# Eleven parts of a Strassen MLP take the plain eight products

## The chip, the cores and the metric

The kernel runs on one core of a Trainium2 chip. The metric is the device time of one execution in microseconds (us), lower is better. Three runs of the kernel before took 2641.0 to 2647.37 us, median 2646.51.

The core's engines each work through their own instructions in order and meet through semaphores: TensorE (PE) multiplies matrices, VectorE (DVE), ScalarE (ACT) and GpSimd (POOL) work on rows, SyncE (SP) and ACT issue DMAs.

## The reference

One layer of a decoder on 2048 prompt tokens and 64 sample tokens, width 1024: attention, then a two-layer MLP, both between norms. The part that matters here:

```python
def ffn_sublayer(x, g_pre, w_up_l, w_down_l, g_post):
    h = rmsnorm(x, g_pre)
    a = jax.nn.relu(jnp.einsum('btd,df->btf', h, w_up_l))
    return x + rmsnorm(jnp.einsum('btf,fd->btd', a * a, w_down_l), g_post)
```

`w_up` is 1024 x 4096, `w_down` 4096 x 1024. The layer's attention output `mix` goes through `w_out`, a norm, and the residual (`x1 = x + rmsnorm(mix @ w_out)`) before it.

## The kernel before, in words

Precision: every factor is split into a rounded part and its rest, `hi` and `lo`, and each product is three matmuls, hi·hi, hi·lo and lo·hi. ACT makes `hi` (a cast), DVE or POOL makes `lo` (a subtraction).

`out_and_mlp` runs after attention. It takes the tokens in four groups of 512 (the last with the 64 samples too), four tiles of 128. A group is 8 parts of 512 hidden columns. A part has:

- four units "up" (0 to 3), each 128 hidden columns: 24 matmuls, relu and square by ACT;
- then the down product of the part, 512 hidden columns x 1024 outputs, by Strassen's scheme: seven units "down" in the order P1, P7, P2, P6, P5, P4, P3. Each is two tiles x 2 blocks x 3 = 12 matmuls (L2171). Four of them need sums of the hidden blocks (`first_sums`, `second_sums`, `third_sum`, L2451, on DVE), all seven their own hi (`high`, L2266, ACT) and lo (`low`, L2479 on DVE, L1988 on POOL). P6, P7, P4 and P5 read sums of weights that an earlier stage stored as `wt`.

`steps()` is the order of all units. The first two up units of the next part stand behind P7 and P6 (`LEADS`). In a group's last part the transposes `h` of the next group's tiles (L2080, two halves each) stand behind the units 2 to 6 (`H_AT`); they and the up units share three PSUM banks (`UP_BANKS`), each to be emptied before it is used again.

Weights: SP loads the raw weights of one or two units at a time into three slots (`load_raw`). ACT's `split_hi` (L2203) and the `split_lo` of POOL (L1983) or DVE (L2485: P7, P6 and P3; in last parts P6) work two units ahead (`AHEAD`); the split weights have three slots (`SPLIT`), so a unit's hi waits until the unit three before it is used.

Sums: a product goes to one of five PSUM banks (`Y_BANKS`, chosen in `BANK`, the least recently used first; P2, P3 and P4 go on in the banks of P1, P5 and P7). DVE adds it to the group's sums (L2511 and L2513) and so frees the bank. P1 and P6 belong to two places: they are collected in `shared` and added at the start of the next group (`share`, L2534 and L2538).

Norms: between the units stand the steps of norm chains, at places given by tables (`POST`, `FIRST`, `ADD`, `PRE`, `SECOND` for the next group's `x1` and `h`; `END`, `SCALE`, `END_ADD`, `OUT` for the output of the group before). For a tile they are: ACT squares (L2275), DVE scales (L2562), POOL adds the residual (L1977), which ACT has loaded (L1864), and ACT stores it (L1870 or L2284). They lie in parts 0 to 2 of group 0 and parts 5 to 7 of groups 1 and 2 (next group), and in parts 0 and 1 of groups 1 to 3 (output). In even parts ACT also issues a copy of 3 MB from cache to cache output, behind up 3 (L118).

Unit names below: (g,p) is part p of group g.

## Time and profile before

| what | value |
|---|---|
| median of three runs | 2646.51 us |
| profiled execution | 2644.41 us, of it span 2642.6 us |
| mean granted clock of TensorE | 0.984 |
| TensorE busy with matmuls | 2522.6 us, 95% of the span |
| DVE, ACT, POOL busy | 1382.9, 1166.3, 1415.2 us |
| largest lines of the chain that ended last | `ml_y` L2171 13%, `ml_up` L2095 to L2097 8% each |
| load of `w_up`, 1024 KB: issue to landing | 6.2 us (median) |
| cache copies, 3060 KB | 11.9 and 13.2 us |

A matmul's record lasts longer than the time to the next one, as they are pipelined; the distance between two starts is what one costs. A line of a timeline has in brackets how long the engine was idle before it and what ended that. The clock is given as a share of full speed: 1.00 is 2.4 GHz, 0.5 is 1.2 GHz.

### The profile page before, as it was taken

What the parts mean: (1) busy time and instruction counts of PE and PEld (TensorE: products, weight loads), DVE (VectorE), ACT (ScalarE), POOL (GpSimd) and SP (SyncE); (2) the same over time, 40 slices, a digit from 0 to 9 for tenths busy, and PEclk for the clock granted to TensorE, in tenths of its full rate; (3) what the DMA queues carried; (4) which work ended last, traced back from release to release, by engine and by line L of the source; (5) the groups of instructions that cost most, each with busy time, mean ns of one, the idle gap of its engine ahead of it and who ended that gap; (6) DMA issues with size and microseconds to landing.
All of it is one profiled execution on the core that took longest, in us unless ns stands there. A gap on an engine that the chain in (4) does not pass through costs nothing.

```text
span 2642.6 us, 35400 instructions
## 1 busy us (share of the span) xinstructions
PE 2522.6 (95%) x13562; PEld 2167.4 (82%) x13562; DVE 1382.9 (52%) x2231; ACT 1166.3 (44%) x2002; POOL 1415.2 (54%) x818
## 2 busy tenths in 40 slices
PE   7999999999999999999998999998999999999995
PEld 6899999899996468778877788777778778889884
DVE  6431221265663225865566554676555476655657
ACT  4000110187775534545454444554544455444443
POOL 1216560068663566665566675666665475554555
PEclk9999999999999999999999999999999999999998
DMA  5316764299988944564556555456555263553452
GB/s 183 112 44 244 264 230 120 83 164 180 166 146 212 295 160 166 193 208 159 167 183 242 176 168 183 151 170 232 173 173 193 99 235 120 198 178 127 142 191 96
DMA packets 297903, 457.65 MB, mean 173 GB/s; under 512 B 81748, under 2 KB 202140, under 8 KB 290776
## 3 DMA queue, kind: packets, MB, share of 16 engines
q1 hardware_dynamic: 270546, 313.71, 41.3%
q10 hardware_dynamic: 14518, 89.43, 9.5%
q0 software_dynamic: 12672, 52.24, 5.9%
q8 instruction: 109, 1.79, 0.3%
q14 instruction: 58, 0.48, 0.1%
HBM read 390.50 MB, written 120.53 MB: 193 GB/s over the span
## 4 chain that ended last, share of the span: by engine, by line
PE 76%; DVE 10%; DMA 5%; POOL 3%; ACT 3%; issue 2%; SPq 0%; ACTq 0%; DVEq 0%; POOLq 0%
PE ml_y L2171 13%; PE ml_up L2095 8%; PE ml_up L2096 8%; PE ml_up L2097 8%; PE ml_y L2128 6%; PE pj_acc L518 6%; PE pj_acc L519 6%; PE pj_acc L520 6%; PE at_o L1187 5%; PE at_turn L1167 2%; POOL ml_w_lo L1983 2%; DVE ml_a_lo L2479 2%; DVE ml_a_lo_raw L2451 2%; DVE ml_w_lo L2485 2%; PE at_score L1156 2%
## 5 line engine op out<-in xcount | busy, mean ns | idle before, releaser
L1983 POOL TENSOR_TENSOR ml_w_lo<-em_raw,ml_w_hi 128x1024 fp32r<-128x1024 f32 x296 | 741.2, 2512 | 635.1 <-ACT ml_w_hi L2203 634.9
L2203 ACT CAST ml_w_hi<-em_raw 128x1024 fp32r<-128x1024 f32 x384 | 401.4, 1046 | 295.8 <-PE ml_y L2171 189.0
L2095 PE MATMUL ml_up<-ml_h_hi,ml_w_hi 128*128 128x512 f32 (+2 forms) x1280 | 457.1, 357 | 23.3 <-POOL ml_w_lo L1983 23.3
L2096 PE MATMUL ml_up<-ml_h_lo,ml_w_hi 128*128 128x512 f32 (+2 forms) x1280 | 453.5, 354 | 0.0
L2097 PE MATMUL ml_up<-ml_h_hi,ml_w_lo 128*128 128x512 f32 (+2 forms) x1280 | 452.6, 354 | 0.0
L2171 PE MATMUL ml_y<-ml_w_hi,ml_a_hi 128*128 128x512 f32 x896 | 358.2, 400 | 34.4 <-DVE em_hx L2513 13.8
L2171 PE MATMUL ml_y<-ml_w_lo,ml_a_hi 128*128 128x512 f32 x896 | 352.6, 393 | 0.0
L2171 PE MATMUL ml_y<-ml_w_hi,ml_a_lo 128*128 128x512 f32 x896 | 352.3, 393 | 0.0
L2095 PEld LDWEIGHTS ml_up<-ml_h_hi,ml_w_hi 128*128 128x128 f32 x1280 | 243.2, 190 | 66.3 <-POOL ml_w_lo L1983 35.3
L518 PE MATMUL pj_acc<-pj_h_hi,pj_w_hi 128*128 128x424 f32 (+1 forms) x800 | 290.3, 363 | 5.6 <-DVE pj_h_lo L736 5.6
L519 PE MATMUL pj_acc<-pj_h_lo,pj_w_hi 128*128 128x424 f32 (+1 forms) x800 | 283.5, 354 | 0.0
L520 PE MATMUL pj_acc<-pj_h_hi,pj_w_lo 128*128 128x424 f32 (+1 forms) x800 | 283.4, 354 | 0.0
L2485 DVE TENSOR_TENSOR ml_w_lo<-em_raw,ml_w_hi 128x1024 fp32r<-128x1024 f32 x88 | 132.1, 1501 | 264.7 <-ACT ml_w_hi L2203 264.4
L2096 PEld LDWEIGHTS ml_up<-ml_h_lo,ml_w_hi 128*128 128x128 f32 x1280 | 243.4, 190 | 30.7
L2097 PEld LDWEIGHTS ml_up<-ml_h_hi,ml_w_lo 128*128 128x128 f32 x1280 | 243.1, 190 | 31.0
L2171 PEld LDWEIGHTS ml_y<-ml_w_hi,ml_a_hi 128*128 128x128 f32 x896 | 170.1, 190 | 83.8 <-DVE em_hx L2513 15.7
L754 DVE SCALAR_TENSOR_TENSOR pj_proj<-pj_acc,pj_scale,pj_rstd_of 128x424 f32<-128x424 f32 (+1 forms) x100 | 65.0, 656 | 311.0 <-PE pj_acc L520 311.0
L2171 PEld LDWEIGHTS ml_y<-ml_w_hi,ml_a_lo 128*128 128x128 f32 x896 | 170.2, 190 | 36.2
L2171 PEld LDWEIGHTS ml_y<-ml_w_lo,ml_a_hi 128*128 128x128 f32 x896 | 170.5, 190 | 33.6
L2479 DVE TENSOR_TENSOR ml_a_lo<-ml_a_lo_raw,ml_a_hi 128x512 fp32r<-128x512 f32 x128 | 166.9, 1304 | 0.1
L2255 ACT ACTIVATE ml_a<-ml_up 128x512 f32<-128x512 f32 (+1 forms) x80 | 41.0, 513 | 279.4 <-PE ml_up L2097 269.6
L518 PEld LDWEIGHTS pj_acc<-pj_h_hi,pj_w_hi 128*128 128x128 f32 x800 | 150.9, 189 | 15.7 <-issue 8.3
(319 smaller groups left out, 4559.8 us busy)
## 6 DMA issues: line engine op xcount, KB each, us to landing
em_raw<-in_w_up SPq DMA_DIRECT2D x64, 1024.0 KB, 6.2
em_raw<-scratch_wt SPq DMA_DIRECT2D x128, 512.0 KB, 4.7
em_raw<-in_w_down SPq DMA_DIRECT2D x96, 512.0 KB, 3.7
out_o_a_k_s<-in_cache_a_k ACTq DMA_DIRECT2D x8, 3060.0 KB, 11.9
out_o_a_v_s<-in_cache_a_v ACTq DMA_DIRECT2D x8, 3060.0 KB, 13.2
em_raw<-scratch_pt SPq DMA_DIRECT2D x34, 512.0 KB, 7.3
pj_work<-in_w_down POOLq DMA_DIRECT2D x16, 1024.0 KB, 6.3
scratch_wt<-pj_work POOLq DMA_DIRECT2D x16, 1024.0 KB, 4.5
```

The costliest lines, as they stand in the source:

```text
L518: pe.matmul(acc[g][:, 0:n], w_hi[:, i % 2, k, :], h_hi[:, k, cols], start=(k == 0), stop=False)
L519: pe.matmul(acc[g][:, 0:n], w_hi[:, i % 2, k, :], h_lo[:, k, cols], start=False, stop=False)
L520: last = pe.matmul(acc[g][:, 0:n], w_lo[:, i % 2, k, :], h_hi[:, k, cols], start=False, stop=(k == DBLK - 1))
L1983: nc.gpsimd.tensor_tensor(split_of(w_lo, n), raw_of(n), f32(split_of(w_hi, n)), ALU.subtract).then_inc(w_lo_ready, 1)
L2095: pe.matmul(out, hi[:, k, :], h_hi[:, k, cols], start=(k == 0), stop=False)
L2096: pe.matmul(out, hi[:, k, :], h_lo[:, k, cols], start=False, stop=False)
L2097: last = pe.matmul(out, lo[:, k, :], h_hi[:, k, cols], start=False, stop=(k == DBLK - 1))
L2128: last = pe.matmul(out, p[:, f, t0:t0 + m], w[:, b, :], start=(f == 0 and p is act_hi and w is hi), stop=(f == DBLK - 1 and p is act_lo))
L2171: last = pe.matmul(out, p[:, SLOT[i], c:c + P], w[:, f, :], start=(i not in ONTO and f == 0 and p is a_hi and w is hi), stop=(f == DF - 1 ...
L2203: nc.scalar.copy(split_of(w_hi, n), raw_of(n)).then_inc(w_hi_ready, 1)
L2479: nc.vector.tensor_tensor(a_lo[:, slot, :], frm, f32(a_hi[:, slot, 0:2 * HT]), ALU.subtract).then_inc(a_lo_by_dve, 1)
L2485: nc.vector.tensor_tensor(split_of(w_lo, n), raw_of(n), f32(split_of(w_hi, n)), ALU.subtract).then_inc(w_lo_by_dve, 1)
```

## The change

In eleven parts the seven products are replaced by the plain eight: parts 0, 1 and 7 of group 0, and parts 0, 5, 6 and 7 of groups 1 and 2. Such a part is four units "plain" of 24 matmuls: unit i computes output half i // 2 from the hidden half i % 2, for all four tiles, with the sums over both hidden halves in the same PSUM banks. DVE adds four tiles after units 1 and 3. There are no sums of blocks, four hi and four lo of the hidden blocks (the lo all by DVE), and all `w_lo` are POOL's. Up units of the next part stand behind plain units 0 and 2. In last parts the `h` of the next group stand ahead of unit 0 and behind units 0, 1 and 2. The weights come as one load for two units. Norm steps keep their tables, and those placed at a product go to the plain unit given in `IN_PLAIN`. The additions of `shared` move from the next group's first up unit to up 2 and 3 of the first plain part behind the last Strassen part of a group: (0,7), (1,5), (2,5).

```diff
-    H_AT = (2, 3, 4, 5, 6)
...
+    PLAIN = ((0, 1, LAST), (0, LAST - 2, LAST - 1, LAST), (0, LAST - 2, LAST - 1, LAST), ())
+    PLAINS = 2 * DF
+    PLAIN_LEADS = (0, 2)
+    PLAIN_H = {0: (1,), 1: (2,), 2: (3, 4)}
+    PLAIN_SLOT = ((SLOT[P1], SLOT[P7]), (SLOT[P2], SLOT[P4]))
+    IN_PLAIN = {P1: 0, P7: 0, P2: 1, P6: 1, P5: 2, P4: 3, P3: 3}
+
+    def is_plain(g, part):
+        return part in PLAIN[g]
+
+    def last_of_seven(g):
+        return max(part for part in range(PARTS) if not is_plain(g, part))
+
+    def first_of_seven(g):
+        return min(part for part in range(PARTS) if not is_plain(g, part))
+
+    def sevens_before(step):
+        return sum(not is_plain(*divmod(at, PARTS)) for at in range(step[1] * PARTS + step[2]))
+
+    def plains_before(step):
+        return step[1] * PARTS + step[2] - sevens_before(step)
...
+                if is_plain(g, part):
+                    if part == LAST and g + 1 < NG:
+                        yield "h", g + 1, 0, 0
+                    for i in range(PLAINS):
+                        yield "plain", g, part, i
+                        if part < LAST and i in PLAIN_LEADS:
+                            yield "up", g, part + 1, PLAIN_LEADS.index(i)
+                        for j in PLAIN_H.get(i, ()):
+                            if part == LAST and g + 1 < NG and j < len(tiles(g + 1)):
+                                yield "h", g + 1, 0, j
+                    continue
...
+        if kind == "plain":
+            return list(range(PROMPT_TILES)) if i % DF == DF - 1 else []
...
+    def unit_at(kind, g, part, i):
+        if kind == "down" and is_plain(g, part):
+            return "plain", g, part, IN_PLAIN[i]
+        return kind, g, part, i
...
+                if kind == "plain":
+                    half = i // DF
+                    sp.dma_start(to.rearrange("p (k c) -> p k c", c=HALF),
+                                 down_v[part][:, :, half * HALF:(half + 1) * HALF]).then_inc(landed, 16)
...
+            def product_plain(n):
+                step = UNITS[n]
+                kind, g, part, i = step
+                half, f0 = divmod(i, DF)
+                wait_lo(pe, n)
+                pe.wait_ge(plain_lo, 4 * plains_before(step) + 2 * (f0 + 1))
+                hi, lo = split_of(w_hi, n), split_of(w_lo, n)
+                for j in range(PROMPT_TILES):
+                    q = sum_at(("plain", g, part, half * DF + DF - 1), j)
+                    if f0 == 0:
+                        pe.wait_ge(y_added, BEFORE[q] + 1)
+                    out, slot = y_ps[BANK[q]][:, :], PLAIN_SLOT[f0][j // PAIRS]
+                    for f in range(DF):
+                        c = f * HT + j % PAIRS * P
+                        for p, w in ((a_hi, hi), (a_hi, lo), (a_lo, hi)):
+                            last = pe.matmul(out, p[:, slot, c:c + P], w[:, f, :], start=(f0 == 0 and f == 0 and p is a_hi and w is hi),
+                                             stop=(f0 == DF - 1 and f == DF - 1 and p is a_lo))
+                    if f0 == DF - 1:
+                        last.then_inc(y_done, 1)
+                    elif j == PROMPT_TILES - 1:
+                        last.then_inc(down_used, 1)
...
-                    act.wait_ge(shared_added, PROMPT_TILES * g + j + 1)
+                    act.wait_ge(y_added, sum_at(("plain", g, LAST, PLAINS - 1), j) + 1)
...
+                        if i == DF and is_plain(g, part):
+                            act.wait_ge(y_done, FIRST_Q[step])
+                            wait_hidden(act, ("up", g, part, DF - 1))
+                            for q in range(2):
+                                high_plain(PLAIN_SLOT[0][q], a[:, q, :, :].rearrange("p f t -> p (f t)"))
...
+            def low_plain(step, his, slot, frm):
+                dve.wait_ge(plain_hi, 4 * plains_before(step) + his)
+                nc.vector.tensor_tensor(a_lo[:, slot, :], frm, f32(a_hi[:, slot, 0:2 * HT]), ALU.subtract).then_inc(plain_lo, 1)
...
+            def add_plain(step, j):
+                kind, g, part, i = step
+                q, half = sum_at(step, j), i // DF
+                dve.wait_ge(y_done, q + 1)
+                add_sum(mixed(g)[:, j, half * HALF:(half + 1) * HALF], y_ps[BANK[q]][:, :], part == 0)
...
+            def share(step):
+                kind, g, part, i = step
+                if i == DF:
+                    dve.wait_ge(y_added, FIRST_Q[step])
+                    for j in range(PAIRS):
+                        share_right(g, j)
+                else:
+                    for j in range(PAIRS):
+                        share_both(g, j)
...
-                        if g and part == 0 and i == 0:
-                            share(g - 1)
-                        if i == DF:
+                        if i == DF and is_plain(g, part):
+                            for q in range(2):
+                                low_plain(step, q + 1, PLAIN_SLOT[0][q], a[:, q, :, :].rearrange("p f t -> p (f t)"))
...
+                        if i == PF - 1 and is_plain(g, part):
+                            for q in range(2):
...
+                        if i >= DF and is_plain(g, part) and part == last_of_seven(g) + 1:
+                            share(step)
+                    elif kind == "plain":
+                        if part == last_of_seven(g) + 1 and i == DF - 1:
+                            dve.wait_ge(shared_added, PROMPT_TILES * (g + 1))
+                        for j in sums_of(step):
+                            add_plain(step, j)
```

Counters of waits that counted parts now count Strassen parts and plain parts apart.

## Rows read from the trace of the kernel before

**Rows 1.** Groups in 1040 to 2642 us: count, busy us, mean ns, idle before, releasers.

```profile
L2095 PE MATMUL ml_up<-ml_h_hi,ml_w_hi 128*128 128x512 f32 (+2 forms) x1280 | 457.1, 357 | 23.3 <-POOL ml_w_lo L1983 23.3
L2171 PE MATMUL ml_y<-ml_w_hi,ml_a_hi 128*128 128x512 f32 x896 | 358.2, 400 | 34.4 <-DVE em_hx L2513 13.8 <-DVE ml_w_lo L2485 8.7 <-DVE em_y L2513 7.6
```

**Rows 2.** Windows: stretch, span us, busy us (count) per engine, granted clock, DMA share, GB/s.

```profile
1185.02:1226.29 41.27, 41.10 (x181) 33.71 (x180) 23.52 (x26) 19.68 (x26) 22.80 (x11) 1.00 0.43 140
1042.66:1099.29 56.63, 54.06 (x229) 43.66 (x228) 34.70 (x34) 32.19 (x50) 34.44 (x14) 0.97 0.58 195
1099.29:1143.48 44.19, 41.69 (x182) 33.55 (x180) 35.16 (x34) 22.36 (x32) 30.57 (x13) 1.00 0.51 177
1350.15:1385.94 35.79, 34.11 (x165) 27.95 (x164) 25.56 (x32) 19.25 (x28) 23.42 (x11) 1.00 0.41 133
1385.94:1449.20 63.26, 55.33 (x230) 44.03 (x228) 38.66 (x39) 30.92 (x46) 38.88 (x19) 0.95 0.66 238
1666.36:1712.20 45.84, 43.33 (x182) 34.70 (x180) 34.60 (x34) 29.03 (x45) 29.88 (x12) 0.96 0.45 149
1712.20:1757.95 45.75, 43.25 (x181) 34.73 (x180) 35.02 (x34) 22.46 (x32) 30.27 (x13) 0.96 0.68 240
1757.95:1794.96 37.01, 34.41 (x166) 27.98 (x164) 26.78 (x32) 19.24 (x28) 23.41 (x11) 1.00 0.40 129
1794.96:1858.73 63.77, 55.41 (x230) 44.09 (x228) 38.66 (x39) 30.89 (x46) 38.84 (x19) 0.95 0.65 235
2085.43:2129.66 44.23, 41.71 (x181) 33.56 (x180) 35.74 (x35) 28.92 (x45) 30.07 (x12) 1.00 0.45 143
2129.66:2177.84 48.18, 43.27 (x181) 34.71 (x180) 36.87 (x36) 25.26 (x38) 33.75 (x14) 0.96 0.69 240
2177.84:2220.51 42.67, 36.81 (x173) 29.73 (x172) 32.26 (x38) 20.60 (x31) 24.35 (x11) 0.96 0.35 115
```

**Rows 3.** Timeline of TensorE: start us, us, instruction, count; clean part, then an h step.

```profile
1226.29 0.39 PE L2095 MATMUL ml_up<-ml_h_hi,ml_w_hi 128*128 128x512 f32 x1
...
1237.17 0.39 PE L2171 MATMUL ml_y<-ml_w_hi,ml_a_hi 128*128 128x512 f32 x1
...
1378.71 1.04 PE L2080 MATMUL ml_up<-all_ident,em_y 128*128 128x128 f32 x8
1379.51 0.48 PE L2171 MATMUL ml_y<-ml_w_hi,ml_a_hi 128*128 128x512 f32 x1
```

**Rows 4.** Timeline, part (0,0), DVE and TensorE: in brackets idle time before, releaser.

```profile
1078.81 3.22 DVE L2562 SCALAR_TENSOR_TENSOR em_y<-em_y,ml_rstd,ml_gain_post 128x1024 f32<-128x1024 f32 x1
...
1082.69 0.80 PE L2171 MATMUL ml_y<-ml_w_hi,ml_a_hi 128*128 128x512 f32 x1 [2.28 <-DVE em_hx L2511]
```

**Rows 5.** Timeline, part (1,0): ACT's queue, POOL, ACT, TensorE.

```profile
1410.06 0.58 ACTq L118 DMA_DIRECT2D out_o_a_k_s<-in_cache_a_k  x1
...
1413.04 0.47 ACTq L1864 DMA_DIRECT2D ml_res<-scratch_x  x1
...
1427.62 2.34 POOL L1977 TENSOR_TENSOR em_hx<-em_hx,ml_res 128x1024 f32<-128x1024 f32 x1 [5.51 <-DMA ml_res<-scratch_x]
...
1430.43 1.05 ACT L2203 CAST ml_w_hi<-em_raw 128x1024 fp32r<-128x1024 f32 x1 [6.07 <-POOL em_hx L1977]
...
1432.65 0.79 PE L2095 MATMUL ml_up<-ml_h_hi,ml_w_hi 128*128 128x512 f32 x1 [5.68 <-POOL ml_w_lo L1983]
```

**Rows 6.** Groups in 1040 to 2642 us: the splits and the relu.

```profile
L1983 POOL TENSOR_TENSOR ml_w_lo<-em_raw,ml_w_hi 128x1024 fp32r<-128x1024 f32 x279 | 697.6, 2508 | 607.8 <-ACT ml_w_hi L2203 607.7
...
L2479 DVE TENSOR_TENSOR ml_a_lo<-ml_a,ml_a_hi 128x512 fp32r<-128x512 f32 x32 | 79.3, 2477 | 12.8 <-ACT ml_a_hi L2266 12.8
...
L2255 ACT ACTIVATE ml_a<-ml_up 128x512 f32<-128x512 f32 (+1 forms) x80 | 41.0, 513 | 279.4 <-PE ml_up L2097 269.6 <-DVE ml_a_lo L2479 9.8
...
L2266 ACT CAST ml_a_hi<-ml_a 128x512 fp32r<-128x512 f32 x32 | 19.7, 614 | 0.0
```

**Rows 7.** Timeline of DVE after group 0: the two wide additions.

```profile
1390.76 2.35 DVE L2538 TENSOR_TENSOR em_hx<-em_hx,ml_shared 128x1024 f32<-128x1024 f32 x2
```

More of the change, by code:

```diff
@@ L1551, in steps @@
                             yield "conv", g + 1, 0, 0
-                    if part == LAST and g + 1 < NG and i in H_AT[0:len(tiles(g + 1))]:
-                        yield "h", g + 1, 0, H_AT.index(i)
     STEPS = list(steps())
-    UNITS = [step for step in STEPS if step[0] in ("op", "up", "down")]
+    UNITS = [step for step in STEPS if step[0] in ("op", "up", "down", "plain")]
     UNIT_OF = {step: n for n, step in enumerate(UNITS)}
@@ L1581, in out_and_mlp @@
         q += len(sums_of(step))
-        used += step[0] == "op" and not sums_of(step)
+        used += step[0] in ("op", "plain") and not sums_of(step)
     def sum_at(step, j):
@@ L1632, in placed @@
                 first = 0 if g == 1 else LAST - 2
-                found.setdefault((kind, g - 1, first + part, i), []).append((g, j))
+                found.setdefault(unit_at(kind, g - 1, first + part, i), []).append((g, j))
         for j in range(len(tiles(0))):
@@ L1642, in placed_end @@
             for j, (kind, part, i) in enumerate(places):
-                found.setdefault((kind, g + 1, part, i), []).append((g, j))
+                found.setdefault(unit_at(kind, g + 1, part, i), []).append((g, j))
         return found
@@ L2018, in _ @@
                 kind, g, part, i = step
-                at = part_of(step)
+                at = sevens_before(step)
                 split_lo(n + AHEAD)
@@ L2136, in wait_operand @@
                 kind, g, part, i = step
-                at = part_of(step)
+                at = sevens_before(step)
                 if i in BY_DVE:
@@ L2179, in _ @@
                     turn_mix(step)
+                elif step[0] == "plain":
+                    product_plain(n)
+                    n += 1
                 elif step[0] == "h":
@@ L2238, in relu @@
                 kind, g, part, i = step
-                at = part_of(step)
-                if i == 0 and at:
-                    act.wait_ge(a_summed, 4 * at)
-                    act.wait_ge(a_lo_by_dve, 5 * (at - 1) + 1)
+                sevens, plains = sevens_before(step), plains_before(step)
+                after_plain = plains and (is_plain(g, part - 1) if part else is_plain(g - 1, LAST))
+                if i == 0 and after_plain:
+                    act.wait_ge(plain_lo, 4 * (plains - 1) + 2)
+                elif i == 0 and sevens:
+                    act.wait_ge(a_summed, 4 * sevens)
+                    act.wait_ge(a_lo_by_dve, 5 * (sevens - 1) + 1)
                 if i == 0 and has_samples(g):
@@ L2266, in high, with high_plain @@
                 nc.scalar.copy(a_hi[:, slot, 0:2 * HT], frm).then_inc(a_hi_done, 1)
+            def high_plain(slot, frm):
+                nc.scalar.copy(a_hi[:, slot, 0:2 * HT], frm).then_inc(plain_hi, 1)
             def high_samples(part, stage):
@@ L2309, in _ @@
                 kind, g, part, i = step
-                at = part_of(step)
+                at = sevens_before(step) if kind in ("up", "down") else 0
                 if step == ("turn", 0, 0, 2):
@@ L2459, in second_sums @@
                 kind, g, part, i = step
[L2460 removed]
+                at = sevens_before(step)
                 by_f = [a_raw[:, s, :].rearrange("p (f t) -> p f t", t=HT) for s in range(DBLK)]
@@ L2471, in third_sum @@
             def third_sum(step):
-                at = part_of(step)
+                at = sevens_before(step)
                 by_f = [a_raw[:, s, :].rearrange("p (f t) -> p f t", t=HT) for s in range(DBLK)]
@@ L2523, in add_down @@
                 elif i in (P1, P6):
-                    add_sum(shared[:, j, :], src, part == 0 and i == P1)
+                    add_sum(shared[:, j, :], src, part == first_of_seven(g) and i == P1)
                 elif i in (P7, P5):
@@ L2538, in share_both @@
                 nc.vector.tensor_tensor(at, at, shared[:, j, :].unsqueeze(1).to_broadcast([P, 2, HALF]), ALU.add).then_inc(shared_added, 1)
-            def share(g):
-                dve.wait_ge(y_added, FIRST_Q[("up", g + 1, 0, 0)])
-                for j in range(PAIRS):
-                    share_right(g, j)
-                for j in range(PAIRS):
-                    share_both(g, j)
+            def share(step):
[4 more added lines that the diff above has]
+                        share_right(g, j)
+                else:
+                    for j in range(PAIRS):
+                        share_both(g, j)
             def samples_done(late):
@@ L2649, in _ @@
                 kind, g, part, i = step
-                at = part_of(step)
+                at = sevens_before(step)
                 if kind == "turn":
@@ L2672, in _ @@
                         norms(step)
-                        if i == PF - 1:
+                        if i == PF - 1 and is_plain(g, part):
+                            for q in range(2):
+                                low_plain(step, q + 3, PLAIN_SLOT[1][q], a_raw[:, KEPT + q, :])
+                        elif i == PF - 1:
                             second_sums(step)
+                        if i >= DF and is_plain(g, part) and part == last_of_seven(g) + 1:
[5 more added lines that the diff above has]
+                            add_plain(step, j)
                     elif kind == "op" and sums_of(step):
```

19 lines of the change are left out of this document (13 added, 6 removed).

## The prediction

> **What bounds the kernel now.** I read the waits by group first, then the windows by stage, then the timeline at the longest waits. The two groups of TensorE with the longest idle time in the MLP stage show who keeps it waiting [rows 1]: the first matmul of an up unit waits 23.3 us in all for POOL's `w_lo`, and that of a product 34.4 us, most of it for sums that DVE has not yet added. The windows cut the stage into stretches: from up unit 2 of a part (up 0 for part 0) to up unit 2 of the next. The first row of [rows 2] is the clean pattern, part 3 of group 0. Its 180 matmuls start 0.2267 us apart (48 of them take 1237.17 - 1226.29 = 10.88 us [rows 3]), so 40.80 of its 41.27 us are matmuls. TensorE is the bound there, and only its own work counts. The other eleven rows are the eleven parts that the change makes plain. They sum to 527.3 us. They hold five stretches of 180 matmuls, three of 228 and three of 132, together 1980 x 0.2267 = 448.8 us, and 13 `h` steps of 0.80 us (1378.71 to 1379.51 [rows 3]), 10.4 us. So 68.1 us of them is neither: 11 x 0.47 = 5.2 us that the clean stretch has as well, and 62.9 us of norm chain. The largest are (1,0) and (2,0): clean, with the two more up units of a part 0, would be 41.27 + 10.88 = 52.15 us, and they take 11.1 and 11.6 more. Then come (2,7) and (2,6).
>
> **How a stall arises.** Two kinds. In (0,0) DVE runs one norm product of 3.22 us, and behind it, in order, stands the sum that frees the bank of P6's second tile: TensorE idles 2.28 us [rows 4], and the granted clock averages 0.97 over that stretch [rows 2], so part of the next matmuls runs at 1.2 instead of 2.4 GHz. In (1,0) ACT issues the cache copy at 1410.06, then the load of a residual tile at 1413.04. POOL, which adds that tile, idles 5.51 us for it until 1427.62. ACT waits 6.07 us for POOL's sum before it can store the row, and only then casts the next `w_hi`; `w_lo` follows, and TensorE idles 5.68 us [rows 5]. Such waits show because a product unit lasts 12 x 0.2267 = 2.72 us: a weight that is split two units ahead has 5.44 us in hand.
>
> **The change, part by part.**
>
> Added matmuls: a plain part has 4 x 24 = 96 where seven products had 84. 11 x 12 = 132, all on TensorE's path and with nothing to hide them: 132 x 0.2267 = +29.9 us. This is certain to within the spacing, since the new matmuls have the form of the old ones.
>
> The Trainium skill, TensorE: Matmul & The Clock Gate, section Back-to-back issue gap, gives about 131 ns for a matmul of 512 columns in a stream of weight loads and matmuls, and 216 ns for one alone. By the first the addition would cost 17.3 us, by the second 28.5. The trace disagrees with the first [rows 3], and the trace decides.
>
> Removed work off TensorE: of each plain part four DVE sums of the operand, one DVE and two POOL `a_lo`, six of 14 sums of the output, and three DVE `w_lo` (one in a last part). ACT makes four `a_hi` instead of seven and four `w_hi` instead of seven. POOL keeps its 8 `w_lo` a part (four up, four product), now in a stretch of 43.5 us: 8 x 2.51 = 20 us [rows 6], with room for a residual sum or two. None of this is worth time by itself. It is worth the stalls that it feeds.
>
> Deeper lookahead: a plain unit lasts 24 x 0.2267 = 5.44 us, so a weight split two units ahead has 10.88 us in hand everywhere. And a plain sum needs its bank back one unit (5.44 us) after it is finished, with the fifth bank taken first, where P6 needed it sooner. A 3.22 us norm product [rows 4] no longer reaches TensorE. I take the (0,0) kind to nothing, and the 0.47 of the clean stretch too: (0,0), (0,1), (1,5), (1,6), (2,5), (2,6) keep 0.1 us each, 0.6 together. Bound from below 0; from above the 2.3 us wait that they have now.
>
> Parts (1,0) and (2,0): the cache copy and the residual load stay in ACT's queue in the same order. The landing decides, so I follow it from the start T of the first product (1407.70). ACT reaches the load somewhat earlier, at T + 4.5 instead of 5.3, as it no longer waits for DVE's sums. Issue to use took 1427.62 - 1413.04 = 14.6 us, so POOL starts its sum at T + 19.1 and ends it at 21.5. It has been waiting at the step of the up lead, and the `w_lo` of the second up lead stands behind it: T + 24.2. TensorE wants that weight after four units, T + 21.8. It waits 2.4 us instead of 5.68. For the clock after a wait of that size, the granted 0.97 over 56.6 us in (0,0) makes 1.7 us, the 1.00 in (0,1) nothing [rows 2]; I add 1.3 and put 3.7 us each, 7.4 together. Bounds: nothing, if the load lands 3 us sooner, and the 11.6 us over of now.
>
> Last parts: `h` 0 now stands ahead of the first plain unit and the others between the units. Only three PSUM banks hold them, so `h` 1 needs a bank that DVE must empty after it has made the operand of the second half: relu and a square of the same size at 0.51 each, the first cast at 0.62 and two `a_lo`, of 2.48 us each where they meet a `w_lo` [rows 6], make up to 6.6 us after up 3, and then comes the split of `h` 0; the bank is wanted at 0.8 + 5.44 = 6.2. In group 0 the two wide additions of the shared product (2.35 us [rows 7]) come in between too. I put 1.0 us for (0,7), 0.3 for (1,7), and 1.5 for (2,7), where `h` 3 and `h` 4 follow each other on the same banks: 2.8 together; bounds 0 and 8. The wait for `h` at the start of the next group disappears, since a 5.44 us unit stands behind the last `h`.
>
> The moved additions of the shared product otherwise hide: `share` in (1,5) and (2,5) runs on DVE under two up units of 10.9 us. The new wait of DVE before its first plain sums is for its own additions and holds nothing. DVE waits in a plain unit for all four sums; behind it stand norm products of the next step, due a unit later. The loads become half as many, one of 1 MB where two of 512 KB stood; they are issued three loads ahead, and no TensorE wait in [rows 1] is for a load, so nothing. Group 3 and the thirteen other Strassen parts of groups 0 to 2 keep their work: 0.
>
> Sum: the eleven stretches lose 68.1 - 0.6 - 7.4 - 2.8 = 57.3 us of waiting and gain 29.9 of matmuls: -27.4. The profiled execution took 2644.4 us (span 2642.6), so 2617.0. It lay 2.1 us under the median of 2646.5; I take half of that: 2618.
>
> **Rivals.**
>
> A, all waits go. The load lands early and DVE is never late: -68.1 + 29.9 = -38.2, 2606 us. For it: the slack doubles everywhere. Against it: the landing chain above.
>
> B, half of the waits stay. DVE and ACT still run the norm chain in order, and whatever is late next shows: -34 + 30, 2640 us. For it: the chain itself is unchanged. Against it: no step of it is longer than the 5.44 us now in hand, but the load.
>
> C, slower. POOL becomes the pacing engine of the norm chain: it adds the residual in order with all eight `w_lo` of a part, and a sum that waits for its load or for DVE holds up the next weight. Its price is what (1,0) shows, 5.68 us of idle plus 2 us for the clock (between the 1.7 above and the 3.2 that 0.95 over 63.3 us makes [rows 2]), in the eight stretches with a residual sum ((0,0), (0,1), (1,0), (1,5), (1,6), (2,0), (2,5), (2,6)): 8 x 7.7 = 62 us, 2644.4 - 68.1 + 29.9 + 62 = 2668 us. It makes the kernel slower from 38.2 / 8 = 4.8 us a stretch on. For it: POOL did wait 5.51 us [rows 5], and in a plain part every `w_lo` is POOL's, where DVE had three of eleven. Against it: only in (1,0) and (2,0) does a cache copy stand ahead of a load that is soon due; in the other six TensorE waited for DVE.
>
> That the change does not do what it says I rule out: the diff's list is 3 + 4 + 4 parts, and the step generator gives each four units of 24.
>
> **How the numbers follow.** Forecast (2608 to 2630): 0.70. A (about 2606): 0.08. B (2630 to 2645): 0.15. C: 0.07. Predicted time 2618. The range goes from A's 2606 to 2636, into B; it leaves out C and over half of B, some 0.16. The measurement tells a change from 0.3%, 7.9 us, so faster means under 2638.6: the forecast, A, and nearly half of B, 0.85. Same: 0.08. Slower: C, 0.07.
>
> **What would show it.** The eleven stretches grow by 12 matmuls each: a plain one without waits lasts 43.5 us (192 x 0.2267), with an `h` step per tile on top in last parts. TensorE's wait for DVE at the product's line falls from 34 us to under 10, and the new line for plain products has next to none. POOL's `w_lo` ends a wait of 2 to 3 us at the second up lead of (1,0) and (2,0), none elsewhere in these parts. The prediction is wrong if stretches without a residual load are over 45 us, if TensorE waits at `h` 1 for more than 2 us, or if the spacing in a plain unit is not 0.227 us.

## The result, and the profile after

The kernel after takes 2617.68 us (median of four runs, 2616.93 to 2623.07), the kernel before 2644.62 (2641.0 to 2647.37): ratio 0.9903, 95% interval 0.9884 to 0.9923. A second series gave 2609.77 against 2644.47, 0.9879 (0.9857 to 0.9902). The profiled execution took 2618.4 us, its span is 2616.3 us (before 2642.6), and the granted clock averages 0.989 (before 0.984). The forecast was 2618.

The windows of the same eleven stretches, in the order and with the columns of [rows 2] without its clean one: (0,0), (0,1), (0,7), (1,0), (1,5), (1,6), (1,7), (2,0), (2,5), (2,6), (2,7).

```profile
1041.68:1096.08 54.40, 54.40 (x241) 45.06 (x240) 16.80 (x20) 27.47 (x44) 31.47 (x12) 1.00 0.57 193
1096.08:1139.60 43.52, 43.52 (x193) 36.05 (x192) 19.51 (x20) 17.76 (x26) 26.60 (x10) 1.00 0.36 121
1345.92:1382.16 36.24, 36.24 (x177) 30.36 (x176) 18.31 (x24) 14.61 (x22) 16.38 (x7) 1.00 0.28 88
1382.16:1442.76 60.60, 56.29 (x241) 46.12 (x240) 22.02 (x21) 26.37 (x40) 35.73 (x16) 0.97 0.64 228
1660.08:1703.60 43.52, 43.52 (x194) 36.04 (x193) 24.91 (x24) 24.53 (x39) 28.34 (x10) 1.00 0.44 145
1703.60:1747.12 43.52, 43.52 (x194) 36.04 (x193) 21.27 (x20) 17.76 (x26) 25.84 (x10) 1.00 0.58 193
1747.12:1783.36 36.24, 36.24 (x178) 30.35 (x177) 14.77 (x20) 14.61 (x22) 14.36 (x6) 1.00 0.27 88
1783.36:1845.23 61.87, 57.27 (x242) 46.88 (x240) 22.38 (x21) 26.37 (x40) 35.65 (x16) 0.94 0.63 224
2070.53:2114.07 43.54, 43.54 (x193) 36.04 (x192) 25.58 (x25) 25.61 (x41) 28.33 (x10) 1.00 0.37 126
2114.07:2157.59 43.52, 43.52 (x193) 36.04 (x192) 24.65 (x22) 19.37 (x31) 30.13 (x11) 1.00 0.66 219
2157.59:2195.49 37.90, 37.32 (x186) 31.02 (x184) 16.98 (x24) 15.26 (x24) 14.37 (x6) 1.00 0.27 86
```

In eight rows span and TensorE's busy time are the same number: it never waited. Six of them (54.40, then 43.52 or 43.54) are nothing but matmuls, 240 or 192 x 0.2267; DVE's busy time in them, 35 to 37 us before, is now 17 to 26. (0,7) and (1,7), 36.24 each, are 144 matmuls, four `h` steps and 0.4 us. Only (1,0), (2,0) and (2,7) hold idle time. The eleven sum to 504.9 us, 22.4 less than before; 0.0 to 7.5 us of each is neither matmuls nor `h` steps, 15.7 in all, where it was 68.1.

The two groups of [rows 1] after the change (the lines have new numbers):

```profile
L2138 PE MATMUL ml_up<-ml_h_hi,ml_w_hi 128*128 128x512 f32 (+2 forms) x1280 | 454.8, 355 | 14.8 <-POOL ml_w_lo L2026 14.8
...
L2214 PE MATMUL ml_y<-ml_w_hi,ml_a_hi 128*128 128x512 f32 x588 | 232.0, 395 | 6.2 <-DVE ml_w_lo L2574 3.9 <-DVE em_y L2602 1.9 <-DVE em_y L2600 0.2
```

The Strassen line's waits fell from 34.4 to 6.2 us, and the line of the plain products (L2234) has none; the waits at `up`, where POOL's `w_lo` is late, only from 23.3 to 14.8. Of the 14.8, 8.9 are two waits, 4.3 us in (1,0) and 4.6 us in (2,0). The timeline of (1,0), queue of ACT, ACT, POOL and TensorE, answers [rows 5]; the first product starts at T = 1403.92:

```profile
1406.27 0.53 ACTq L118 DMA_DIRECT2D out_o_a_k_s<-in_cache_a_k  x1
1407.95 0.41 ACTq L1902 DMA_DIRECT2D ml_res<-scratch_x  x1
...
1427.92 1.04 ACT L2271 CAST ml_w_hi<-em_raw 128x1024 fp32r<-128x1024 f32 x1 [10.66 <-POOL em_hx L2020]
...
1425.10 2.35 POOL L2020 TENSOR_TENSOR em_hx<-em_hx,ml_res 128x1024 f32<-128x1024 f32 x1 [8.47 <-DMA ml_res<-scratch_x]
...
1427.74 4.70 POOL L2026 TENSOR_TENSOR ml_w_lo<-em_raw,ml_w_hi 128x1024 fp32r<-128x1024 f32 x2
...
1430.15 0.50 PE L2138 MATMUL ml_up<-ml_h_hi,ml_w_hi 128*128 128x512 f32 x1 [4.31 <-POOL ml_w_lo L2026]
```

Counted from T, the load was issued 1.3 us earlier than before (T + 4.0 for T + 5.3), but POOL got its data only 17.15 us after the issue, 14.6 before. So POOL, with more slack around it, idles longer (8.47 us for 5.51), and ACT behind it 10.66 us.

### The profile page after: what moved, and what is told of

Its sections match the earlier page's. It is cut to its first block, busy times and chain, and to the rows that moved or that the text cites. A ratio compares the mean times of both kernels' runs of the same rounds, so it can differ in the third digit from the quotient of the medians.

```text
span 2616.3 us, 35292 instructions
## 1 busy us (share of the span) xinstructions
PE 2533.8 (97%) x13694; PEld 2187.4 (84%) x13694; DVE 1229.0 (47%) x2083; ACT 1114.4 (43%) x1936; POOL 1362.9 (52%) x790
## 4 chain that ended last, share of the span: by engine, by line
PE 82%; DMA 5%; POOL 4%; DVE 4%; ACT 2%; issue 1%; SPq 1%; ACTq 0%; DVEq 0%; POOLq 0%
PE ml_y L2214 10%; PE ml_up L2138 9%; PE ml_up L2139 9%; PE ml_up L2140 9%; PE ml_y L2234 8%; PE ml_y L2171 6%; PE pj_acc L518 6%; PE pj_acc L519 6%; PE pj_acc L520 6%; PE at_o L1187 4%; PE at_turn L1167 2%; POOL ml_w_lo L2026 2%; DMA ml_res<-scratch_x 2%; PE at_score L1156 1%; DMA dk_k_new<-scratch_kv 1%
## 5 line engine op out<-in xcount | busy, mean ns | idle before, releaser
L2026 POOL TENSOR_TENSOR ml_w_lo<-em_raw,ml_w_hi 128x1024 fp32r<-128x1024 f32 x290 | 725.4, 2508 | 665.6 <-ACT ml_w_hi L2271 665.5
L2271 ACT CAST ml_w_hi<-em_raw 128x1024 fp32r<-128x1024 f32 x351 | 366.8, 1045 | 327.8 <-PE ml_y L2214 135.4
L2138 PE MATMUL ml_up<-ml_h_hi,ml_w_hi 128*128 128x512 f32 (+2 forms) x1280 | 454.8, 355 | 14.8 <-POOL ml_w_lo L2026 14.8
L2214 PE MATMUL ml_y<-ml_w_hi,ml_a_hi 128*128 128x512 f32 x588 | 232.0, 395 | 6.2 <-DVE ml_w_lo L2574 3.9
L2214 PE MATMUL ml_y<-ml_w_lo,ml_a_hi 128*128 128x512 f32 x588 | 230.3, 392 | 0.0
L2214 PE MATMUL ml_y<-ml_w_hi,ml_a_lo 128*128 128x512 f32 x588 | 230.1, 391 | 0.0
L2574 DVE TENSOR_TENSOR ml_w_lo<-em_raw,ml_w_hi 128x1024 fp32r<-128x1024 f32 x61 | 76.6, 1255 | 194.2 <-ACT ml_w_hi L2271 193.9
L518 PEld LDWEIGHTS pj_acc<-pj_h_hi,pj_w_hi 128*128 128x128 f32 x800 | 150.8, 188 | 15.6 <-issue 8.3
L520 PEld LDWEIGHTS pj_acc<-pj_h_hi,pj_w_lo 128*128 128x128 f32 x800 | 150.9, 189 | 2.7
L519 PEld LDWEIGHTS pj_acc<-pj_h_lo,pj_w_hi 128*128 128x128 f32 x800 | 150.9, 189 | 2.2
L2602 DVE TENSOR_TENSOR em_y<-ml_y,em_y 128x512 f32<-128x512 f32 x166 | 110.1, 685 | 70.9 <-PE ml_y L2234 35.2
L1216 ACT ACTIVATE em_y<-em_y,em_hx 128x256 f32<-128x256 f32 (+3 forms) x288 | 136.8, 517 | 14.8 <-DVE em_hx L1274 12.2
```

The costliest lines, as they stand in the source:

```text
L518: pe.matmul(acc[g][:, 0:n], w_hi[:, i % 2, k, :], h_hi[:, k, cols], start=(k == 0), stop=False)
L519: pe.matmul(acc[g][:, 0:n], w_hi[:, i % 2, k, :], h_lo[:, k, cols], start=False, stop=False)
L520: last = pe.matmul(acc[g][:, 0:n], w_lo[:, i % 2, k, :], h_hi[:, k, cols], start=False, stop=(k == DBLK - 1))
L1216: last = nc.scalar.activation(row, row, ACT.Exp, bias=stage[:, j % STAGES, tile["out"], VW:VW + 1], scale=-1.0)
L2026: nc.gpsimd.tensor_tensor(split_of(w_lo, n), raw_of(n), f32(split_of(w_hi, n)), ALU.subtract).then_inc(w_lo_ready, 1)
L2138: pe.matmul(out, hi[:, k, :], h_hi[:, k, cols], start=(k == 0), stop=False)
```

## The experiments

Lines and names in the diffs are those of the kernel each starts from. Each ratio is to the kernel before, in the same series.

**The copy behind the load: e1_copy_later, e2_before_copy_later.** The first starts from the kernel after, the second has the same edit in the kernel before: the cache copy of part 0 is issued a part later.

```diff
-                    if kind == "up" and i == PF - 1 and part % 2 == 0:
+                    if kind == "up" and i == PF - 1 and part in (1, 2, 4, 6):
```

> The changed kernel with each group's cache copy of part 0 issued in part 1 (behind its up 3) instead. Theory (the 3 MB copy stands in ACT's queue ahead of the residual load that POOL must add, and POOL's next w_lo stands behind that sum): the two waits of TensorE at the second up lead of (1,0) and (2,0), 4.31 and 4.60 us in the profile, go with the slow clock behind them; the two stretches fall from 60.6 and 61.9 us to about 54.4 each, the kernel from 2617.7 to about 2605 us. Rival (POOL's residual sums are late in any case, through the load's own duration or the norm chain ahead of it): over 2 us of wait stay in each, the time is 2611 us or more.

> The kernel before with the same move of the copy and nothing else. Theory: of the 11.1 and 11.6 us that (1,0) and (2,0) take over a clean stretch, the copy's share is the 5.68 and 6.14 us of wait and some 2 us of clock each; it goes and 3 us of other waits stay: 2644.6 minus 14 to 16, about 2630 us. Rival (these waits come from the 5.44 us of slack of 2.72 us units, whatever the load does): less than 5 us gained, 2640 us or more.

Measured: e1 2604.96 us, ratio 0.9857 (0.9822 to 0.9891); e2 2631.86, 0.997 (0.9952 to 0.9989). Windows of e1, (1,0), (2,0) and (3,0), and its wait in (3,0); then windows of e2, (0,7), (1,0) and (3,0).

```profile
1379.68:1434.08 54.40, 54.40 (x241) 45.07 (x240) 22.80 (x21) 26.28 (x40) 35.84 (x16) 1.00 0.56 196
1772.50:1826.90 54.40, 54.40 (x242) 45.06 (x240) 22.80 (x21) 26.29 (x40) 35.84 (x16) 1.00 0.57 197
2177.56:2245.47 67.91, 63.29 (x390) 57.74 (x388) 39.86 (x39) 33.65 (x71) 40.76 (x18) 0.97 0.47 162
...
PE ml_y L2214 <- DVE em_y L2602: 4.4, 1, 4.4
```

```profile
1348.41:1387.70 39.29, 34.47 (x165) 27.98 (x164) 29.01 (x32) 19.22 (x28) 22.81 (x11) 1.00 0.37 121
1387.70:1446.48 58.78, 53.10 (x229) 42.43 (x228) 41.77 (x39) 30.89 (x46) 40.56 (x19) 1.00 0.58 198
...
2208.36:2277.19 68.83, 64.22 (x389) 58.44 (x389) 44.73 (x42) 32.94 (x71) 41.30 (x18) 0.95 0.47 161
```

In e1 both stretches fall to 54.40, matmuls alone: all the idle time that was left in (1,0) and (2,0) after the change goes with the copy ahead of the load. Group 3, which has no plain part, pays: TensorE waits 4.4 us for DVE in (3,0), which was 63.5 us before. The timelines show where they come from: first two instructions of DVE and POOL's work beside them in e1, then the same two of DVE, with POOL's work, in e3 (the next experiment), where (3,0) takes 62.2 us.

```profile
2218.08 3.44 DVE L2574 TENSOR_TENSOR ml_w_lo<-em_raw,ml_w_hi 128x1024 fp32r<-128x1024 f32 x1
2221.63 3.18 DVE L2660 SCALAR_TENSOR_TENSOR em_hx<-em_hx,ml_rstd,ml_gain 128x1024 f32<-128x1024 f32 x1
...
2215.17 5.27 POOL L2020 TENSOR_TENSOR em_hx<-em_hx,ml_res 128x1024 f32<-128x1024 f32 x2
2220.39 3.34 POOL L2026 TENSOR_TENSOR ml_w_lo<-em_raw,ml_w_hi 128x1024 fp32r<-128x1024 f32 x1
```

```profile
2216.15 1.21 DVE L2574 TENSOR_TENSOR ml_w_lo<-em_raw,ml_w_hi 128x1024 fp32r<-128x1024 f32 x1
2217.47 1.28 DVE L2660 SCALAR_TENSOR_TENSOR em_hx<-em_hx,ml_rstd,ml_gain 128x1024 f32<-128x1024 f32 x1
...
2213.24 2.43 POOL L2020 TENSOR_TENSOR em_hx<-em_hx,ml_res 128x1024 f32<-128x1024 f32 x1
```

DVE does the same work in the same order, but in e1 each of the two starts while POOL is at work and ends 1.1 us after POOL's instruction does (2221.52 after 2220.44, 2224.81 after 2223.73). Together they take 4.1 us more than in e3. In e1 POOL adds two residual tiles in a row there, in e3 one, and then it idles.

e2 gained 8.4 us in its series, between the theory's 14 to 16 and the rival's 5. (1,0) drops only 4.5 us and stays 6.6 over clean, so in the Strassen form taking the copy away ends less than half of the trouble. (3,0) loses 5.3 us, by the same wait of 4.4 us as in e1, and (0,7) 3.5, waiting there for DVE's sums and `w_lo`. With units of 2.72 us, a wait removed in one place came out in another.

**The addition behind the next unit: e3_add_later, e5_before_add_later.** The copy stays; the third residual sum of a part 0 moves from the second up lead behind P5, and its store behind P4. e3 starts from the kernel after, e5 from the kernel before.

```diff
-    END_ADD = (("up", 0, 3), ("up", 1, 0), ("up", 1, 0), ("down", 0, P5))
-    OUT = (("down", 0, P7), ("down", 0, P2), ("down", 0, P6), ("down", 0, P4))
+    END_ADD = (("up", 0, 3), ("up", 1, 0), ("down", 0, P5), ("down", 0, P5))
+    OUT = (("down", 0, P7), ("down", 0, P2), ("down", 0, P4), ("down", 0, P4))
```

> The changed kernel with the copy where it was, but POOL's sum of the third output tile two units later (behind the w_lo of the last plain unit) and its store in the last plain unit. The load is as late as before. Theory (what costs is that a w_lo stands behind the waiting sum on POOL): the waits of TensorE in (1,0) and (2,0) go all the same, about 2605 us, with POOL still idle for the load. Rival (the copy itself slows something else, such as the raw weights): the waits stay, about 2617 us.

> The kernel before, all Strassen, with POOL's sum of the third output tile moved from up 0 of part 1 to behind P6's place (at P5) and its store to P4, as in the run e3 of the changed kernel. Theory (the two long waits are a matter of POOL's order, not of Strassen): (1,0) and (2,0) fall from 63.3 and 63.8 us to 55 to 57, the time by 13 to 16 us to about 2630 us (against 2644.6). Rival (a product of 2.72 us leaves too little time in any order): the waits turn up at other units, less than 6 us gained.

Measured: e3 2598.52 us, 0.9834 (0.9799 to 0.9868); e5 2622.49, 0.993 (0.9914 to 0.9947). Windows of e3, (1,0) and (3,0), and two rows of its POOL timeline in (1,0); then the window of e5, (1,0).

```profile
1377.43:1431.83 54.40, 54.40 (x241) 45.08 (x240) 22.11 (x21) 26.38 (x40) 36.01 (x16) 1.00 0.71 254
...
2175.63:2237.85 62.22, 61.73 (x389) 56.59 (x388) 36.27 (x39) 33.77 (x71) 39.16 (x18) 1.00 0.63 218
...
1416.89 2.40 POOL L2026 TENSOR_TENSOR ml_w_lo<-em_raw,ml_w_hi 128x1024 fp32r<-128x1024 f32 x1 [1.88 <-ACT ml_w_hi L2271]
1419.51 2.41 POOL L2020 TENSOR_TENSOR em_hx<-em_hx,ml_res 128x1024 f32<-128x1024 f32 x1 [0.22 <-DMA ml_res<-scratch_x]
```

```profile
1382.53:1438.85 56.32, 53.14 (x230) 42.41 (x228) 39.61 (x39) 30.89 (x46) 42.01 (x19) 1.00 0.73 262
```

In e3 the load (issued at 1403.22, used 16.3 us later) lands as late as ever, and TensorE doesn't notice: the `w_lo` now stands ahead of the sum. So a late transfer costs nothing once no urgent `w_lo` stands behind the sum that waits for it; an early one (e1) is enough too, but not needed. (3,0) gains here instead of losing. In e5 the same two lines take 6.9 us off (1,0) and 7.5 off (2,0), some 14 us, with no plain part at all; the time fell by 15.6 in its series. 4.2 us over clean stay in (1,0), of which 3.0 are waits: 1.6 for DVE's sums and 1.4 for POOL's `w_lo` at another unit.

**The price of a plain part: e4_plain_clean.** From the kernel after, the parts 3, 4 and 5 of group 0, which have no norm chain, go plain too.

```diff
-    PLAIN = ((0, 1, LAST), (0, LAST - 2, LAST - 1, LAST), (0, LAST - 2, LAST - 1, LAST), ())
+    PLAIN = ((0, 1, 3, 4, 5, LAST), (0, LAST - 2, LAST - 1, LAST), (0, LAST - 2, LAST - 1, LAST), ())
```

> The changed kernel with parts 3, 4 and 5 of group 0 plain too. These had no norm work: 41.27 us with 0.47 of waiting. Theory: 12 more matmuls of 0.2267 us are all paid for, less the 0.47: 3 x (2.72 - 0.47) = +6.8 us over the changed kernel, 2624.4 us, each stretch 43.52 us. Rival (the matmuls are cheaper in a stream, 0.131 us each, as the page Back-to-back issue gap of TensorE: Matmul & The Clock Gate in the Trainium skill has it): 3 x (1.57 - 0.47) = +3.3 us.

Measured: 2619.91 us, 0.9908 (0.9871 to 0.9946). The window of (0,4):

```profile
1219.63:1263.15 43.52, 43.52 (x193) 36.07 (x192) 9.91 (x12) 15.07 (x20) 19.17 (x8) 1.00 0.50 169
```

41.26 us with seven products, 43.52 with eight: 2.25 = 12 x 0.2267 less the 0.47 of waiting that goes too. All three parts show it to 0.01 us. The whole time, 2.2 us over the 2617.68 above and in another series, is too coarse for their 6.8 us: in the profile (2,0) alone took 2.8 us less than in the kernel after.

**Longer units or less work for DVE: e7_dve_as_before, e8_strassen_light.** e7 starts from the kernel after and gives DVE back a load like the one it had: three `w_lo` a part and 11 subtractions of 512 columns, placed at the part's units and sums (`more` is called with 1 to 3 of them).

```diff
+            return (kind == "down" and i in (LO_BY_DVE_LAST if part == LAST else LO_BY_DVE)) or (kind == "plain" and i in ((1,) if part == LAST else (0, 2, 3)))
...
+            def more(n):
...
+                for _ in range(n):
+                    stepped(nc.vector.tensor_tensor(lower[:], gain_post[0:DEC, 0:2 * HT], gain_pre[0:DEC, 0:2 * HT], ALU.subtract))
```

e8 starts from the kernel before: short units stay, DVE's `w_lo` in eight parts of groups 1 and 2 shrinks to two columns (the rest of it is left out of the product).

```diff
+                c = 1 if is_light(*UNITS[n][1:3]) else HALF
+                nc.vector.tensor_tensor(split_of(w_lo, n)[:, :, 0:c], raw_of(n)[:, :, 0:c], f32(split_of(w_hi, n)[:, :, 0:c]), ALU.subtract).then_inc(w_lo_by_dve, 1)
```

> The changed kernel with DVE's load put back in the eleven plain parts: eleven more DVE subtractions of 64x512 a part (for the sums and the a_lo that went) and w_lo of three plain units (of one in a last part) on DVE instead of POOL. The extra subtractions write a spare tile, so the output stays as it was. Slack theory (a unit of 5.44 us covers a late DVE): the stretches without a cache copy ahead, (0,0), (0,1), (1,5), (1,6), (2,5), (2,6), stay within 0.5 us of 54.4 and 43.5, and the time within 4 us of 2617.7. Work theory (they got faster because DVE had less to do): waits of 2 us and more come back in them, 3 to 5 us each, 2635 us or more.

> The kernel before, Strassen everywhere, with DVE's w_lo in parts 0, 5, 6 and 7 of groups 1 and 2 cut from 1024 columns to two (a part of the weights' lo is left out), some 4 to 6 us of DVE time less a part. Work theory: the waits for DVE at P6, 2.3 us each and 4.5 in (2,6), go; (1,5), (1,6), (2,5) fall to 41.3 to 42 us, the time by 10 us or more. Slack theory (in its strong form: only the longer unit helps): these waits stay within 0.5 us of what they were, the time within 4 us.

Measured: e7 2610.07 us, 0.9889 (0.9869 to 0.9909); e8 2616.58, 0.9914 (0.9894 to 0.9933). Windows of e7, (1,5) and (2,6); then of e8, (1,5), (1,6) and (2,6).

```profile
1658.50:1702.02 43.52, 43.52 (x193) 36.05 (x192) 33.52 (x35) 24.43 (x39) 20.29 (x8) 1.00 0.43 145
...
2106.94:2150.46 43.52, 43.52 (x193) 36.05 (x192) 33.51 (x36) 19.48 (x32) 19.60 (x8) 1.00 0.66 219
```

```profile
1660.18:1701.82 41.64, 41.46 (x182) 33.56 (x180) 31.54 (x34) 29.01 (x45) 29.23 (x12) 1.00 0.45 149
1701.82:1743.33 41.51, 41.33 (x181) 33.64 (x180) 30.27 (x34) 22.47 (x32) 30.05 (x13) 1.00 0.77 270
...
2108.78:2156.13 47.35, 44.26 (x181) 35.70 (x180) 33.19 (x36) 25.23 (x38) 32.94 (x14) 0.93 0.71 255
```

DVE is busy 33.5 us in these two (31.3 to 34.1 in the other 43.5 us stretches, 27.4 in (0,0)), nearly as in [rows 2] with 34.6 to 36.9, and TensorE waits for nothing. A longer unit is enough, with a DVE nearly as busy as before. POOL is relieved at the same time, so this run says nothing of POOL. But e8 shows that it isn't the only way: 3 to 5 us less on DVE and short units, and (1,5) and (1,6) come to 41.6 and 41.5, a few tenths over clean. My reason "a deeper lookahead" holds as a sufficient cause; as the only one it falls. (2,6) is the cleanest comparison: with DVE busy 33.2 us and short units (e8) TensorE still waits 2.91 us, with 33.5 us and long ones (e7) not at all.

**Which parts have to be plain: e6_few_plain.** From e3, with only (0,7), (1,7), (2,6) and (2,7) plain.

```diff
-    PLAIN = ((0, 1, LAST), (0, LAST - 2, LAST - 1, LAST), (0, LAST - 2, LAST - 1, LAST), ())
+    PLAIN = ((LAST,), (LAST,), (LAST - 1, LAST), ())
```

> The changed kernel with the sum moved as in e3, but plain only in (0,7), (1,7), (2,6) and (2,7). Theory (a part is worth making plain where its waits, with the slow clock behind them, are over 2.72 us): the seven parts that are Strassen again, (0,0), (0,1), (1,0), (1,5), (1,6), (2,0), (2,5), take 0.7 to 2.3 us more each, in all 6 to 14 us more than e3, 2605 to 2612 us. Rival (the waits of 2.3 us are paid off by the 12 matmuls saved): within 3 us of e3's 2598.5 us.

Measured: 2618.87 us, 0.9921 (0.9904 to 0.9938), where e3 has 0.9834: some 20 us more. The seven parts that are Strassen again take 13.2 us of it in the profiles (337.3 in e3, 350.5 here), within the 6 to 14 expected. What was not expected is (2,6), 6.7 us more. The profiled execution also reached the MLP 4.7 us later than e3's, with the same code ahead of it. Windows of (1,6) and (2,6), then the timeline of DVE and TensorE in (2,6).

```profile
1704.46:1748.66 44.20, 41.73 (x182) 33.56 (x180) 35.20 (x34) 22.45 (x32) 30.46 (x13) 1.00 0.71 249
...
2111.38:2161.64 50.26, 46.32 (x193) 37.80 (x192) 34.85 (x26) 20.54 (x32) 30.37 (x12) 0.93 0.60 199
```

```profile
2126.34 5.70 DVE L2568 TENSOR_TENSOR ml_a_lo<-ml_a_lo_raw,ml_a_hi 128x512 fp32r<-128x512 f32 x2
2131.96 4.55 DVE L2633 TENSOR_TENSOR em_hx<-em_hx,ml_shared 128x1024 f32<-128x1024 f32 x2
...
2136.62 3.23 DVE L2660 SCALAR_TENSOR_TENSOR em_y<-em_y,ml_rstd,ml_gain_post 64x1024 f32<-64x1024 f32 x1
...
2139.96 3.42 DVE L2660 SCALAR_TENSOR_TENSOR em_y<-em_y,ml_rstd,ml_gain_pre 128x1024 f32<-128x1024 f32 x1
2143.31 2.47 DVE L2602 TENSOR_TENSOR em_hx<-ml_y,em_hx 128x512 f32<-128x512 f32 x4
...
2144.04 0.79 PE L2234 MATMUL ml_y<-ml_w_hi,ml_a_hi 128*128 128x512 f32 x1 [3.94 <-DVE em_hx L2602]
```

A plain (2,6) that is the first plain part takes 50.3 us, more than the Strassen (2,6) with 48.2. The additions of the shared product move with the first plain part. In (2,6) they fall between two `a_lo` and two norm products, 16.9 us of DVE in a row, and the banks come free 3.94 us late. In the kernel after they stand in (2,5), and (2,6) waits for nothing. So the choice of the first plain part has a price of its own.

**Giving POOL DVE's `w_lo` instead: e10_pool_lo.** From e9 below; (0,0), (0,1), (1,5) and (1,6) go back to seven products, with only P6's `w_lo` left on DVE.

```diff
-            return kind == "down" and i in (LO_BY_DVE_LAST if part == LAST else LO_BY_DVE)
+            return kind == "down" and i in (LO_BY_DVE_LAST if part == LAST or (g, part) in ((0, 0), (0, 1), (1, 5), (1, 6)) else LO_BY_DVE)
```

> e9 with (0,0), (0,1), (1,5) and (1,6) Strassen again, but there only P6's w_lo on DVE and those of P7 and P3 on POOL. Work theory (DVE was late at P6 for what it had to do; the run e8 showed 41.5 us for such a part without DVE's w_lo): the four stretches take 41.3 to 42 us (52.5 for (0,0)) instead of 43.5 (54.4), 6 to 8 us less than e9. Rival (POOL, with ten w_lo and two a_lo in a part and 5.44 us of slack, is late in its place): they take 43.5 us or more, no gain on e9.

Measured: 2603.93 us, 0.9852 (0.9832 to 0.9872), against e9's 0.9809. The window of (0,1), and two waits of TensorE in (0,0).

```profile
1089.31:1135.41 46.10, 43.51 (x180) 34.80 (x181) 35.04 (x31) 22.31 (x32) 37.92 (x15) 0.96 0.46 158
```

```profile
1071.13 0.50 PE L2214 MATMUL ml_y<-ml_w_hi,ml_a_hi 128*128 128x512 f32 x1 [2.28 <-DVE em_hx L2600]
...
1089.31 0.50 PE L2138 MATMUL ml_up<-ml_h_hi,ml_w_hi 128*128 128x512 f32 x1 [1.31 <-POOL ml_w_lo L2026]
```

DVE is still late by 2.28 us, and POOL, now busy 37.9 of 46.1 us, is late beside it. DVE was not relieved: it is busy 35.04 us with 31 instructions, where (0,1) before had 35.16 with 34 [rows 2]. The two `w_lo` that went took 1.23 us each, and two norm products that took 1.28 and 1.29 us before now take 3.25 and 3.23, each beside an instruction of POOL. Nor did the run take away what e8 took: P6's `w_lo`, 3.43 us beside POOL's work in (0,0), still stands with a norm product of 3.23 ahead of the late sum. So handing P7's and P3's `w_lo` to POOL brings nothing. Handing over P6's as well was not tried.

**The order of loads and sums, with and without plain parts: e9_copies_and_add, e12_strassen_tuned.** e9 is e3 with the copy of part 2 issued in part 3; e12 has both edits on the kernel before.

```diff
-                    if kind == "up" and i == PF - 1 and part % 2 == 0:
+                    if kind == "up" and i == PF - 1 and part in (0, 3, 4, 6):
```

> The changed kernel with the sum moved as in e3 and the cache copies of part 2 issued in part 3 instead (those of parts 0, 4 and 6 as they were). Theory (the waits of (1,2) and (2,2), where part 3's inputs of the merge are loaded behind the copy of part 2, are of the same kind as those of (1,0)): (1,2) and (2,2) fall from 43.4 and 45.4 us to under 42, the time by 3 to 5 us below e3's 2598.5, ratio to the kernel before 0.982. Rival: the loads are late by themselves, ratio 0.983 to 0.984.

> The kernel before, all Strassen, with e9's two other changes (POOL's sum later, part 2's cache copies in part 3). It shows what the plain parts are worth once the loads are out of the way. Theory (what plain removes are the waits for DVE at P6 and the h steps, 2.5 us each with their clock, which stay here): the eleven stretches take 56.5 and 44.2 to 48.2 us as in e5, (1,2) and (2,2) 41.3, ratio to the kernel before 0.990 to 0.993, some 25 us over e9's 2592. Rival (the waits for DVE depend on the copies too): ratio under 0.987.

Measured: e9 2592.17 us, 0.9809 (0.9788 to 0.983), the best; e12 2619.2, 0.9897 (0.9878 to 0.9917). Windows of e9, (1,0) and (1,2); then of e12, (0,7) and (1,0).

```profile
1380.29:1434.69 54.40, 54.40 (x241) 45.05 (x240) 22.34 (x21) 26.38 (x40) 35.96 (x16) 1.00 0.71 254
1477.01:1518.27 41.26, 41.09 (x182) 33.71 (x180) 23.82 (x28) 19.77 (x27) 28.95 (x17) 1.00 0.51 170
```

```profile
1345.19:1387.20 42.01, 37.19 (x165) 30.25 (x164) 29.35 (x32) 19.32 (x28) 22.82 (x11) 0.92 0.35 113
1387.20:1443.54 56.34, 53.17 (x230) 42.44 (x228) 39.60 (x39) 30.90 (x46) 41.96 (x19) 1.00 0.74 266
```

(1,2) and (2,2) lose their waits for the `w_lo` of DVE: 6.3 us together against e3. The order alone gives 1.0% on the kernel before, the plain parts on top of it another 0.9% (0.9809 / 0.9897 = 0.9911), within the noise what they gave without it (0.9879 and 0.9903): the two gains add up. Stretch by stretch they are not the same gain. The eleven stretches differ by 22.4 us between before and after, and by 28.4 between e12 and e9. In (0,7) and (1,7) e12 takes 42.0 and 39.3 us, 8.5 more together than the kernel before. Whether e12's order brings that, or the one execution, is not shown.

**The kernel after once more: e11_after_again.**

> The changed kernel as it is, beside the two above on one chip, for the size of the change itself: ratio 0.990 by the forecast and the first measurement, within 0.002.

Measured: 2609.77 us, 0.9879 (0.9857 to 0.9902). Of the eleven stretches nine are the same to 0.01 us; (1,0) took 58.18 and (2,0) 60.99, 3.3 us less together, so only the two with the load vary. The rest of the 8.2 us by which this profile's span is shorter lies outside of them: 4.2 ahead of the MLP and 1.8 in (2,2), less 1.2 that (3,7) took more. One kernel in two executions differs by that much.

## Why the prediction was right, and where it was not

**Added matmuls, +29.9: right.** e4 measures them alone: a part's matmuls go from 40.80 to 43.52 us, 2.72 more. With the 131 ns of the Trainium skill, TensorE: Matmul & The Clock Gate, section Back-to-back issue gap, the estimate would have been 17.3 us. No stretch here runs at that rate, and the trace's 0.2267 us held in every plain stretch without a wait.

**The (0,0) kind, 0.6 us forecast: 0.0 measured.** All six stretches are matmuls to 0.02 us. The lookahead that I named as cause is enough (e7), but not needed (e8). The sum didn't depend on that.

**(1,0) and (2,0), 7.4 forecast: 13.7 measured (6.2 and 7.5).** This is the term that was mis-sized. The mechanism was right: copy, load, POOL's sum, `w_lo` (e1 takes the first away, e3 changes the order of the last two; both end the wait). The step that failed is "issue to use took 14.6 us, so POOL starts its sum at T + 19.1". ACT did issue the load at T + 4.0, and I added the old duration to the new issue. But that duration wasn't the load's own: without the copy (e1) the load landed 6.0 us after its issue, and with it soon after the copy. The copy went out at T + 2.35 as before, took 15.6 us, and the sum started 3.2 us after it had landed, at T + 21.2; before it was at T + 19.9, 2.4 us after the copy's landing. (Between the two ACT also issues the store of a finished row, 512 KB.) From there the chain is as forecast: the weight wanted at T + 21.9 (21.8 forecast) was ready 5.0 us after POOL's start. So TensorE waited 4.31 and 4.60 us, for 2.4. The matmuls behind the waits ran at the lower clock for a time, which cost 1.9 and 2.9 us (busy 56.29 and 57.27 for 54.40), where I had 1.3. How far the term was off depends on the execution: e11, the same kernel, has waits of 3.49 and 3.59 us, and with the clock 3.8 and 6.6 us, 10.4 together. There the load was used 16.3 and 16.4 us after its issue. Both profiles are over the 7.4.

**Last parts, 2.8 forecast: 2.1 measured.** 0.4, 0.4 and 1.3 for 1.0, 0.3 and 1.5.

**The sum.** The eleven stretches: -27.4 forecast, -22.4 measured; the miss of 5.0 is the 6.3 of (1,0) and (2,0) less small gains. The span fell by 26.3 because 3.9 us went elsewhere, which I had put at 0: (2,2) is 1.3 us shorter, (3,7) 1.2, and the MLP started 1.0 us earlier. So the hit on the total owes 4 to 5 us to luck. None of the three looks like work of the change. The MLP's start lay between 1031 and 1044 us in runs whose code ahead of it is the same. (3,7), from its third up unit to the end of the span, takes 65.2 us before and 64.0 after, but 64.0 also in e2, which has no plain part, and 65.2 in e11, which is the kernel after. (2,2) took 43.2 us in e11 and 45.0 in the first profile. The second series lies 8 us under the forecast for reasons of the same kind.

**The rivals.** A, all waits go, fails through the load alone; e3 shows its state, with (1,0) and (2,0) at 54.40. Half of the waits staying (B) did not happen: 23% stayed. C, POOL as the pacing engine, came in two of its eight stretches, (1,0) and (2,0), and there it cost 6.2 and 7.5 us, near its price of 7.7. That is the mis-sized term above. The other six had no late load. e10 shows that POOL does become late, at 37.9 busy of 46.1 us; in the plain stretches of 43.5 us it is busy 26 to 30.
